# Mixer input tiles of a hybrid encoder trunk: three 256-wide products per weight block turned into one of 512 and one of 256, with the halves joined by ScalarE and VectorE

## The chip, the core and the metric

One core of a Trainium2 chip runs the whole kernel in one launch. The metric is the device time of an execution in microseconds (us). The engines are TensorE (PE, with its weight loads shown as PEld), VectorE (DVE), ScalarE (ACT), GpSimd (POOL) and SyncE (SP), which here only issues DMAs.

## The reference, cut to what matters

Two layers are computed over 256 tokens of 1024 channels. In each, the normalised input is projected once, and the columns of the projection feed attention (q, k, v), the Hyena mixer (`hy_in`) and the gates:

```
hn = rmsnorm(x, norm1_g[l])
proj = hn @ w_in[l]
q, k, v, hy_in, gates = jnp.split(proj, splits, axis=-1)
...
u = short_conv(hy_in, hy_conv_w[l], hy_conv_b[l])   # width 3, zero-padded at both ends
x0, x1, vv = jnp.split(u, 3, axis=-1); z = vv * x1
y = (fft_conv(z, h_fwd) + flip(fft_conv(flip(z), h_bwd)) + z * skip) ; b_out = y * x0
...
x = x + merged @ w_out[l]
x = x + peer(rmsnorm(x, norm2_g[l]), ...)
```

`hy_in` has 1536 channels, which are 12 tiles of 128. They alone are touched by the change.

## The kernel before, in words

All weights arrive as a stream of 128x1024 tiles through a ring of four slots. Products keep the accuracy of float32 by splitting both operands into a high and a low part: for every weight tile ACT writes the high half-tiles (`high_half`, called by `high_parts`, profile line L488), POOL subtracts to get the low ones (`low_parts`, L425), and PE then forms high x high, high x low and low x high. In `product` (L1449) these are three matmuls of 256 columns for each of the 8 blocks of a tile: L1452, L1454, L1456, so 24 in a tile. `contract` (L1462) does a tile and `project` (L1491) adds the wait for a free PSUM bank. `wide_tile` (L1472) is the other form, used before the change for the query tiles and the late expert tiles only: one matmul of 512 columns multiplies the high weights with the high and the low activations side by side (L1479), one of 256 adds low weights x high activations (L1481). It leaves the result in two halves of a bank, which somebody must add.

The order of the work is written out by hand on each engine, and each engine does its own list in order. The stretch that matters runs once a layer. PE's list is: 8 q/k tiles, the v tiles, then mixer tiles 0 and 1, `spread_scales`, mixer tiles 2 and 3, four matmuls for the filter taps (L1602), mixer tiles 4 to 6, four spectrum matmuls (L1613, the last of which waits for `bias_ready`), mixer tiles 7 and 8, the scores of heads 0 and 1 (`head_pair`, L1623), mixer tiles 9 to 11. After that comes a loop over 8 heads: gate tile 2h, a wait for the probabilities of head h, their four transposes (L1642), gate tile 2h+1, then either the scores of the next two heads or the product with the values (L1656). Later come the up projections, the output projection, the queries and the experts, which take most of the layer.

Tiles are numbered m for the banks: the mixer's tile n is m = 8 + n and lies in bank m % 4. A bank is free again when ACT has copied the tile four before it. ACT does this in `hyena_in` (L660), through `copy_tile` (L531, the copy is L534): wait for the tile on PE (`tile_wait`), make the high parts of the tile two ahead, then copy the 256 columns into `u_pad`, a buffer with a zero column at each end of a row. Between mixer tiles 9 and 10 ACT loads the table for Exp (L524) and between and behind tiles 10 and 11 it does the exponentials of heads 0 and 1 (`head_exp`, L698). In the gates' loop it takes a tanh of each gate tile out of its bank (L692).

DVE's list in this stretch is: w3 sums (L1063, L1064), `normalise_qk` for 4 pairs (L1045), the filters (L1072), the mask copied to PSUM (L1081) and added to the biases of 8 heads (L1083, then `bias_ready`), the spectrum (L1092, L1094), `conv(0)` and `conv(1)`, `head_scores` of heads 0 and 1 (L1110, L1114), `conv(2)` and `conv(3)`, then `normalise_probs(0)` (L1120, L1122), whose end releases the first transposes. The other eight convs stand between the heads behind it. A `conv` (L1096) is one TENSOR_SCALAR (L1100) and two SCALAR_TENSOR_TENSORs (L1102, L1104) on a row of `u_pad`, each waiting for the one before.

The code of the wait that sets when a mixer or gate tile may start:

```
def project(tile, m, wait=None, parts=(act_hi, act_lo)):
    if m >= 4:
        pe.wait_ge(tile_copied.sem, tile_copied.at(l, m - 3))
    contract(bank[m % 4][:, 0:S], 0, tile, wait=wait, parts=parts).then_inc(tile_done.sem, 1)
```

## Time and profile before

| | us |
|---|---|
| median of 3 runs | 2042.89 |
| lowest and highest | 2041.94, 2043.87 |
| the profiled execution, its own time | 2044.56 |
| the profiled execution, its span | 2042.7 |
| PE busy | 2032.7 of the span (100%) |
| PEld, POOL, DVE, ACT busy | 1807.5, 1605.7, 1278.4, 1079.1 |

The span runs from the first to the last instruction; the execution's own time is 1.86 us longer than its span. PE is busy throughout, so the time falls when PE's list gets shorter and rises with every wait that PE has to take. Matmuls overlap in the pipeline: one is recorded as 0.28 us long, while the next starts 0.12 us after it. What PE's work costs is therefore read from the distance between starts, not from the durations. Instructions of the other engines carry their duration, and a wait inside an instruction (for a port) makes it look longer.

### The profile page before, as it was taken

The page shows a single profiled execution, that of the slowest core. Times are in us where ns is not written, and L with a number is a line of the kernel's source. Part 1 is how long each engine was busy: PE and PEld are TensorE (multiplying, and loading weights), DVE is VectorE, ACT ScalarE, POOL GpSimd, SP SyncE. Part 2 cuts the span into 40 slices and gives each one's busy share as a digit, 9 for nine tenths or more (in the row PEclk, how much of TensorE's full clock was granted, in tenths as well). Part 3 has the DMA queues.
Part 4 walks back from the last instruction along what each step waited for, and adds up shares of the span by engine and source line. Part 5 has one row for each costly group of instructions (what it writes and reads, how often), then busy time and mean ns, then how long its engine had stood idle before and what let it go on. Part 6 is the DMA issues. An engine that isn't in the chain of part 4 may idle for free.

```text
span 2042.7 us, 43879 instructions
## 1 busy us (share of the span) xinstructions
PE 2032.7 (100%) x13412; PEld 1807.5 (88%) x13412; DVE 1278.4 (63%) x2655; ACT 1079.1 (53%) x2321; POOL 1605.7 (79%) x1316
## 2 busy tenths in 40 slices
PE   9999999999999999999999999999999999999999
PEld 8998899998888888888889898999988888888887
DVE  6776589778888333333377664996888873333333
ACT  6563654554444555555565546555444445555554
POOL 6776978887777888888877668788877778888886
PEclk9999999999999999999999999999999999999999
DMA  8543545554444555555684436555544445555554
GB/s 260 176 145 124 206 155 185 181 169 154 150 147 151 189 192 190 193 195 194 195 227 163 145 128 204 159 181 183 165 154 150 148 150 192 192 195 194 191 192 153
DMA packets 103393, 358.39 MB, mean 175 GB/s; under 512 B 11745, under 2 KB 16803, under 8 KB 103077
## 3 DMA queue, kind: packets, MB, share of 16 engines
q1 hardware_dynamic: 102612, 355.14, 53.1%
q10 hardware_dynamic: 720, 2.44, 0.4%
q8 instruction: 38, 0.62, 0.1%
q14 instruction: 23, 0.18, 0.0%
HBM read 356.49 MB, written 1.05 MB: 175 GB/s over the span
## 4 chain that ended last, share of the span: by engine, by line
PE 94%; DVE 3%; ACT 1%; POOL 1%; issue 1%; DMA 0%; SPq 0%; DVEq 0%; POOLq 0%; ACTq 0%
PE bank L1819 34%; PE bank L1479 15%; PE bank L1452 9%; PE bank L1456 9%; PE bank L1454 9%; PE bank L1481 8%; PE bank L1759 4%; POOL w_lo L425 1%; PE bank L1738 1%; PE bank L1699 1%; PE bank L1690 1%; DVE arena L1122 1%; DVE arena L1104 1%; DVE arena L1100 0%; ACT w_hi L488 0%
## 5 line engine op out<-in xcount | busy, mean ns | idle before, releaser
L425 POOL TENSOR_TENSOR w_lo<-ring,w_hi 128x512 fp32r<-128x512 f32 x1048 | 1404.1, 1356 | 345.8 <-ACT w_hi L488 345.2
L488 ACT ACTIVATE w_hi<-ring 128x512 fp32r<-128x512 f32 x1312 | 754.0, 621 | 377.7 <-PE bank L1456 326.9
L425 DVE TENSOR_TENSOR w_lo<-ring,w_hi 128x512 fp32r<-128x512 f32 x256 | 236.6, 924 | 450.2 <-ACT w_hi L488 450.0
L1452 PE MATMUL bank<-act_parts,w_hi 128*128 128x256 f32 x1600 | 458.9, 287 | 0.1
L1454 PE MATMUL bank<-act_parts,w_hi 128*128 128x256 f32 x1600 | 452.8, 283 | 0.0
L1456 PE MATMUL bank<-act_parts,w_lo 128*128 128x256 f32 x1600 | 452.7, 283 | 0.0
L1819 PE MATMUL bank<-w_hi,e_hi 128*128 128x512 f32 x1024 | 399.0, 390 | 0.2
L1819 PE MATMUL bank<-w_hi,e_lo 128*128 128x512 f32 x1024 | 398.5, 389 | 0.0
L1819 PE MATMUL bank<-w_lo,e_hi 128*128 128x512 f32 x1024 | 398.5, 389 | 0.0
L1479 PE MATMUL bank<-act_parts,w_hi 128*128 128x512 f32 x1088 | 385.9, 399 | 0.0
L1452 PEld LDWEIGHTS bank<-act_parts,w_hi 128*128 128x128 f32 x1600 | 306.9, 192 | 8.9 <-issue 7.2
L1454 PEld LDWEIGHTS bank<-act_parts,w_hi 128*128 128x128 f32 x1600 | 307.0, 192 | 1.0 <-issue 1.0
L1456 PEld LDWEIGHTS bank<-act_parts,w_lo 128*128 128x128 f32 x1600 | 306.9, 192 | 0.0
L1481 PE MATMUL bank<-act_parts,w_lo 128*128 128x256 f32 x1088 | 301.9, 277 | 0.0
L793 ACT ACTIVATE e_hi<-arena 128x256 fp32r (+1 forms) x256 | 106.8, 418 | 315.8 <-PE bank L1819 315.8
L453 POOL TENSOR_TENSOR e_lo<-arena,e_hi 128x256 fp32r<-128x256 f32 x256 | 190.8, 746 | 71.2 <-ACT e_hi L793 71.1
L1479 PEld LDWEIGHTS bank<-act_parts,w_hi 128*128 128x128 f32 x1088 | 204.1, 188 | 44.4
L1819 PEld LDWEIGHTS bank<-w_hi,e_hi 128*128 128x128 f32 x1024 | 192.2, 188 | 41.1 <-POOL e_lo L453 1.0
L1819 PEld LDWEIGHTS bank<-w_hi,e_lo 128*128 128x128 f32 x1024 | 192.2, 188 | 39.9
L1819 PEld LDWEIGHTS bank<-w_lo,e_hi 128*128 128x128 f32 x1024 | 192.2, 188 | 39.7
L1481 PEld LDWEIGHTS bank<-act_parts,w_lo 128*128 128x128 f32 x1088 | 204.6, 188 | 0.0
L799 ACT ACTIVATE norm_tmp<-bank 128x256 f32<-128x256 f32 x136 | 52.2, 384 | 238.7 <-PE bank L1481 238.7
(227 smaller groups left out, 2342.4 us busy)
## 6 DMA issues: line engine op xcount, KB each, us to landing
ring<-stream SPq DMA_DIRECT2D x654, 512.0 KB, 3.3
arena<-rpb_in SPq DMA_DIRECT2D x8, 512.0 KB, 7.9
arena<-dft_in SPq DMA_DIRECT2D x4, 512.0 KB, 6.0
arena<-subkeys ACTq DMA_DIRECT2D x2, 1024.0 KB, 7.0
xT<-x_in SPq DMA_DIRECT2D x4, 256.0 KB, 6.6
ring<-stream SPq DMA_DIRECT2D x4, 256.0 KB, 6.7
arena<-w_in SPq DMA_DIRECT2D x2, 512.0 KB
arena<-decay_in SPq DMA_DIRECT2D x2, 512.0 KB
```

Source lines behind the costliest of these rows:

```text
L425: eng.tensor_tensor(w_lo[:, part_, :], ring[:, tile % RING, half * HT:(half + 1) * HT], w_hi[:, part_, :].bitcast(F32), ALU.subtract).then ...
L453: pool.tensor_tensor(e_lo[:, n % AHEAD, :], experts[:, bass.ds(i * RING + n, 1), :].rearrange("p a t -> p (a t)"), e_hi[:, n % AHEAD, :].b ...
L488: nc.scalar.activation(w_hi[:, 2 * (tile % AHEAD) + half, :], ring[:, tile % RING, half * HT:(half + 1) * HT], ACT.Copy).then_inc(hi_ready ...
L793: nc.scalar.activation(e_hi[:, n % AHEAD, :], experts[:, bass.ds(i * RING + n, 1), :].rearrange("p a t -> p (a t)"), ACT.Copy).then_inc(e_ ...
L799: nc.scalar.activation(u_lo[:, n % 2, :], bank[n % 2][:, S:2 * S], ACT.Copy).then_inc(u_lo_ready.sem, 1)
L1452: T.matmul(out_, weights(w_hi, tile, j), hi[:, k, :], start=start, stop=False, skip_group_check=True)
L1454: T.matmul(out_, weights(w_hi, tile, j), lo[:, k, :], start=False, stop=False, skip_group_check=True)
L1456: return T.matmul(out_, weights(w_lo, tile, j), hi[:, k, :], start=False, stop=stop, skip_group_check=True)
L1479: T.matmul(out_[:, 0:2 * S], weights(w_hi, tile, k), both[:, :, k, :], start=(k == 0), stop=False, skip_group_check=True)
L1481: ins = T.matmul(out_[:, 0:S], weights(w_lo, tile, k), both[:, 0, k, :], start=False, stop=(k == KT - 1), skip_group_check=True)
L1759: ins = T.matmul(bank[2 + n % 2][:, t * NK:(t + 1) * NK], onehot_i[:, n % 2, t // 2, :, t % 2], weighted_j[:, n % 2, t // 2, c, :, t % 2], ...
L1819: ins = T.matmul(bank[4 + 2 * half + tt][:, :], e_[:, n % AHEAD, tokens], w_[:, part_, :], start=first and w_ is w_hi and e_ is e_hi, stop ...
```

## The change

Each of the 12 mixer tiles goes through `wide_tile` with both activation halves side by side. ACT, at the place where it copied the result, now copies the low half (columns 256 to 511 of the bank) into the row of `u_pad`. DVE gets 12 new instructions, `add_mix(n)`: wait for that copy, add the other half from PSUM onto the row. A bank of a mixer tile is free again when DVE has added, no longer when ACT has copied, and `conv(n)` waits for the add. The adds are put at fixed places of DVE's list: 0 and 1 ahead of `normalise_qk`, 2 and 3 behind it, 4 ahead of the mask, 5 between the biases of heads 4 and 5, 6 ahead of the spectrum, 7 behind `conv(0)`, 8 behind `conv(1)`, 9 behind `head_scores(1)`, 10 behind `conv(2)`, 11 behind `conv(3)`. `wide_tile` raises `tile_done` as `project` did.

```diff
--- before.py
+++ after.py
@@ -259,7 +259,9 @@
         ffn_done = sig("ffn_done", 2)
         arg_ready = sig("arg_ready", 2)
         sin_done = sig("sin_done", 2)
-        tile_copied = sig("tile_copied", 36)
+        tile_copied = sig("tile_copied", 24)
+        mix_low_ready = sig("mix_low_ready", 12)
+        mix_added = sig("mix_added", 12)
         q_lo_ready = sig("q_lo_ready", 2 * PH)
         q_sum = sig("q_sum", 2 * PH)
         q2_ready = sig("q2_ready", 2 * PH)
@@ -528,10 +530,11 @@
                     assert n_split[0] == tile + AHEAD
                     split_next()
 
-                def copy_tile(tile, m, dst):
-
-                    tile_wait(tile)
-                    nc.scalar.activation(dst, bank[m % 4][:, 0:S], ACT.Copy).then_inc(tile_copied.sem, 1)
+                def low_of_mix(n):
+
+                    tile_wait(T_HY + n)
+                    nc.scalar.activation(u_pad[:, n, 1:S + 1], bank[n % 4][:, S:2 * S], ACT.Copy
+                                         ).then_inc(mix_low_ready.sem, 1)
 
                 def raw_high(n, k, src):
 
@@ -658,7 +661,7 @@
                         norm_high(1, ((0,), (1, 2), (3,))[m - 4])
 
                 def hyena_in(n):
-                    copy_tile(T_HY + n, 8 + n, u_pad[:, n, 1:S + 1])
+                    low_of_mix(n)
 
                 def sine(n, dst):
                     act.wait_ge(arg_ready.sem, arg_ready.at(l, n))
@@ -1038,6 +1041,12 @@
                                        ).then_inc(v_scale_ready.sem, 1)
                 normalised(1, lambda s: None)
 
+                def add_mix(n):
+
+                    dve.wait_ge(mix_low_ready.sem, mix_low_ready.at(l, n + 1))
+                    row = u_pad[:, n, 1:S + 1]
+                    V.tensor_tensor(row, bank[n % 4][:, 0:S], row, ALU.add).then_inc(mix_added.sem, 1)
+
                 def normalise_qk(n):
 
                     dve.wait_ge(spread_done.sem, spread_done.at(l, n + 1))
@@ -1063,8 +1072,12 @@
                 V.tensor_tensor(w3_sd[:, 0, :], w3[:, 0, :], w3[:, 1, :], ALU.add)
                 V.tensor_tensor(w3_sd[:, 1, :], w3[:, 0, :], w3[:, 1, :], ALU.subtract
                                 ).then_inc(w3_ready.sem, 1)
+                add_mix(0)
+                add_mix(1)
                 for n in range(4):
                     normalise_qk(n)
+                add_mix(2)
+                add_mix(3)
 
                 for n in range(4):
                     sd, tt = n // TT, n % TT
@@ -1078,12 +1091,16 @@
 
                 dve.wait_ge(tables_in.sem, tables_in.at(l, tables_in.per_layer))
                 dve.wait_ge(filters_ready.sem, filters_ready.at(l, 4))
+                add_mix(4)
                 link(V.tensor_copy(mask_ps, mask))
                 for h in range(NH):
+                    if h == 5:
+                        add_mix(5)
                     ins = V.tensor_tensor(bias[:, h, :, :], bias[:, h, :, :],
                                           mask_ps.unsqueeze(1).to_broadcast([P, TT, S]), ALU.add)
                 ins.then_inc(bias_ready.sem, 1)
                 dve.wait_ge(bias_ready.sem, bias_ready.at(l, 1))
+                add_mix(6)
 
                 for ri in range(2):
                     dve.wait_ge(even_kept.sem, even_kept.at(l, ri + 1))
@@ -1095,7 +1112,7 @@
 
                 def conv(n):
 
-                    dve.wait_ge(tile_copied.sem, tile_copied.at(l, 8 + n + 1))
+                    dve.wait_ge(mix_added.sem, mix_added.at(l, n + 1))
                     w = C_CW + 3 * n
                     link(V.tensor_scalar(u[:, n, :], u_pad[:, n, 1:S + 1], col[:, w + 1:w + 2],
                                          col[:, C_CB + n:C_CB + n + 1], ALU.mult, ALU.add))
@@ -1126,11 +1143,16 @@
                     ins.then_inc(probs_ready.sem, 1)
 
                 conv(0)
+                add_mix(7)
                 conv(1)
+                add_mix(8)
                 head_scores(0)
                 head_scores(1)
+                add_mix(9)
                 conv(2)
+                add_mix(10)
                 conv(3)
+                add_mix(11)
                 tiles = [4, 8, 5, 9, 6, 10, 7, 11]
                 normalise_probs(0)
                 for p in range(NH // 2):
@@ -1488,11 +1510,24 @@
                         pe.wait_ge(raw_ready.sem, raw_ready.at(l, (n - 1) * KT + k + 1))
                     return wait
 
+                def bank_free(m):
+
+                    if 4 <= m < 12:
+                        pe.wait_ge(tile_copied.sem, tile_copied.at(l, m - 3))
+                    elif 12 <= m < 24:
+                        pe.wait_ge(mix_added.sem, mix_added.at(l, m - 11))
+                    elif m >= 24:
+                        pe.wait_ge(tile_copied.sem, tile_copied.at(l, m - 15))
+
                 def project(tile, m, wait=None, parts=(act_hi, act_lo)):
 
-                    if m >= 4:
-                        pe.wait_ge(tile_copied.sem, tile_copied.at(l, m - 3))
+                    bank_free(m)
                     contract(bank[m % 4][:, 0:S], 0, tile, wait=wait, parts=parts).then_inc(tile_done.sem, 1)
+
+                def mix_tile(n):
+
+                    bank_free(8 + n)
+                    wide_tile(bank[n % 4], 0, T_HY + n, both_acts)
 
                 def mean_square(n):
 
@@ -1583,15 +1618,15 @@
                             rows = slice(e * FFN, (e + 1) * FFN)
                             ins = T.matmul(bank[5][rows, 0:P], w2[rows, :], h1[rows, :], start=True, stop=True)
                         ins.then_inc(ffn_done.sem, 1)
-                project(T_HY, 8)
-                project(T_HY + 1, 9)
+                mix_tile(0)
+                mix_tile(1)
                 pe.wait_ge(qk_scale_ready.sem, qk_scale_ready.at(l, 1))
                 pe.wait_ge(arg_ready.sem, arg_ready.at(l, 2))
                 pe.wait_ge(v_ready.sem, v_ready.at(l, 2))
                 pe.wait_ge(taps_in.sem, taps_in.at(l, taps_in.per_layer))
                 spread_scales()
-                project(T_HY + 2, 10)
-                project(T_HY + 3, 11)
+                mix_tile(2)
+                mix_tile(3)
 
                 pe.wait_ge(sin_done.sem, sin_done.at(l, 2))
                 pe.wait_ge(w3_ready.sem, w3_ready.at(l, 1))
@@ -1602,7 +1637,7 @@
                     T.matmul(bank[4 + n][:, :], h2[rows, :], w3_sd[rows, sd, :], start=True, stop=True
                              ).then_inc(taps_done.sem, 1)
                 for n in range(4, 7):
-                    project(T_HY + n, 8 + n)
+                    mix_tile(n)
 
                 pe.wait_ge(filters_ready.sem, filters_ready.at(l, 4))
                 pe.wait_ge(tables_in.sem, tables_in.at(l, tables_in.per_layer))
@@ -1625,13 +1660,13 @@
                             if qt:
                                 ins.then_inc(scores_done.sem, 1)
 
-                project(T_HY + 7, 15)
-                project(T_HY + 8, 16)
+                mix_tile(7)
+                mix_tile(8)
                 pe.wait_ge(spec_ready.sem, spec_ready.at(l, 2))
                 head_pair(0)
-                project(T_HY + 9, 17)
-                project(T_HY + 10, 18)
-                project(T_HY + 11, 19)
+                mix_tile(9)
+                mix_tile(10)
+                mix_tile(11)
                 for h in range(NH):
                     project(T_GATE + 2 * h, 20 + 2 * h)
                     pe.wait_ge(probs_ready.sem, probs_ready.at(l, h + 1))
@@ -1670,7 +1705,7 @@
                     for j in (0, 1):
                         m = 2 * n + j
                         if m < 4:
-                            pe.wait_ge(tile_copied.sem, tile_copied.at(l, 36))
+                            pe.wait_ge(tile_copied.sem, tile_copied.at(l, 24))
                         else:
                             pe.wait_ge(up_used.sem, up_used.at(l, m - 3))
                         parts_ready(0, T_UP + n, j)
```

## Rows read from the trace of the kernel before

**Rows 1.** The page: busy time by engine, and the chain that ended last by engine

```profile
PE 2032.7 (100%) x13412; PEld 1807.5 (88%) x13412; DVE 1278.4 (63%) x2655; ACT 1079.1 (53%) x2321; POOL 1605.7 (79%) x1316
...
PE 94%; DVE 3%; ACT 1%; POOL 1%; issue 1%; DMA 0%; SPq 0%; DVEq 0%; POOLq 0%; ACTq 0%
```

**Rows 2.** Waits, 94.9 to 149.6 us: who, for whom, total, times, longest

```profile
PEld bank L1642 <- DVE arena L1122: 0.5, 2, 0.3
```

**Rows 3.** Timeline of PE: start, duration, line; narrow and wide tiles, scores, transposes

```profile
70.04 0.28 PE L1452 MATMUL bank<-act_parts,w_hi 128*128 128x256 f32 x1
...
72.92 3.60 PE L1613 MATMUL bank<-arena 128*128 128x512 f32 x8
...
94.88 0.60 PE L1642 MATMUL bank<-mats,arena 128*128 128x128 f32 x4
...
109.92 0.66 PE L1642 MATMUL bank<-mats,arena 128*128 128x128 f32 x4
...
221.96 0.40 PE L1479 MATMUL bank<-raw_parts,w_hi 128*128 128x512 f32 x1
...
224.73 0.40 PE L1479 MATMUL bank<-raw_parts,w_hi 128*128 128x512 f32 x1
```

**Rows 4.** Timeline of ACT: copies of mixer tiles 7, 9, 10 and 11

```profile
80.55 0.36 ACT L534 ACTIVATE arena<-bank 128x256 f32<-128x256 f32 x1
...
87.56 0.37 ACT L534 ACTIVATE arena<-bank 128x256 f32<-128x256 f32 x1
...
90.44 0.37 ACT L534 ACTIVATE arena<-bank 128x256 f32<-128x256 f32 x1
...
93.32 0.36 ACT L534 ACTIVATE arena<-bank 128x256 f32<-128x256 f32 x1
```

**Rows 5.** Timeline of DVE: an add from PSUM, biases, scores, convs 2 and 3, head 0

```profile
48.40 0.42 DVE L1058 TENSOR_TENSOR arena<-bank,norm_tmp 128x256 f32<-128x256 f32 x1
...
67.32 4.87 DVE L1083 TENSOR_TENSOR arena<-arena,bank 128x512 f32<-128x512 f32 x8
...
83.44 0.69 DVE L1110 SCALAR_TENSOR_TENSOR arena<-bank,arena 128x512 f32<-128x512 f32 x1 [1.66 <-PE bank L1623]
...
86.08 0.40 DVE L1100 TENSOR_SCALAR arena<-arena,cols_sb 128x256 f32<-128x256 f32 x1
86.52 0.48 DVE L1102 SCALAR_TENSOR_TENSOR arena<-arena,cols_sb 128x256 f32<-128x256 f32 x1
...
87.57 1.27 DVE L1100 TENSOR_SCALAR arena<-arena,cols_sb 128x256 f32<-128x256 f32 x1
88.87 1.40 DVE L1102 SCALAR_TENSOR_TENSOR arena<-arena,cols_sb 128x256 f32<-128x256 f32 x1
90.31 1.41 DVE L1104 SCALAR_TENSOR_TENSOR arena<-arena,cols_sb 128x256 f32<-128x256 f32 x1
92.03 0.17 DVE L1120 RECIPROCAL soft<-soft 128x2 f32<-128x2 f32 x1 [0.32 <-ACT arena L698]
92.23 2.18 DVE L1122 TENSOR_SCALAR arena<-arena,soft 128x256 f32<-128x256 f32 x2
```

**Rows 6.** Timeline of POOL: low parts of the weight tiles, 80 to 96 us

```profile
83.07 2.55 POOL L425 TENSOR_TENSOR w_lo<-ring,w_hi 128x512 fp32r<-128x512 f32 x2 [0.16 <-ACT w_hi L488]
87.21 8.35 POOL L425 TENSOR_TENSOR w_lo<-ring,w_hi 128x512 fp32r<-128x512 f32 x6 [1.59 <-ACT w_hi L488]
```

**Rows 7.** PE's clock: windows (busy, PEclk, DMA share, GB/s), then two matmuls of it

```profile
7.00:10.90 3.90, 2.24 (x16) 1.00 1.05 377
10.90:14.40 3.50, 3.16 (x15) 0.53 0.73 238
...
12.90 0.41 PE L1454 MATMUL bank<-raw_lo,w_hi 128*128 128x256 f32 x1
13.11 0.41 PE L1456 MATMUL bank<-raw_hi,w_lo 128*128 128x256 f32 x1
```

**Rows 8.** The second layer: head 0 on DVE

```profile
1105.97 0.17 DVE L1120 RECIPROCAL soft<-soft 128x2 f32<-128x2 f32 x1 [0.32 <-ACT arena L698]
```

## The prediction

> **What bounds the kernel now.** I read the page first, for who is busy and what chain ends last: PE is busy for 100% of the span and is 94% of the chain [rows 1]. So the time is PE's list plus PE's waits, and a change is worth what it takes out of or puts into those. Then I asked for the waits in the stretch around the change. Until the end of the mixer tiles PE has none that counts, and in the gates' loop it waits for DVE only twice, for 0.5 us together, 0.3 at most [rows 2]. Such a small wait in a stretch where DVE has no pause says the two are level: DVE delivers the probabilities just when PE comes for them. The timelines of PE, ACT, DVE and POOL [rows 3 to 6] then give the order of events, in microseconds of the first layer; the second repeats it, 1013.94 us later at head 0 (DVE starts head 0 at 92.03 and 1105.97, both times after 0.32 us of waiting [rows 5, 8]). I work out one layer and double it.
>
> **The gain on PE.** A narrow tile runs from 70.04 to 72.92, which is 2.88 us for 24 matmuls, 0.120 each [rows 3]. Eight steps of the wide form, one matmul of 512 columns and one of 256, take 224.73 - 221.96 = 2.77 us [rows 3]. Both stream 768 columns a step; the wide form saves one of three starts. So a mixer tile becomes 0.107 us shorter, twelve 1.28 us, both layers 2.57 us. That is the most that this change can win. It is 0.13%, under the 0.2% (4.1 us) that a measurement of this kernel can tell from no change.
>
> The Trainium skill, in "TensorE: Matmul & The Clock Gate", section "Back-to-back issue gap", gives 262 cycles of 2.4 GHz for 256 columns and 518 for 512, by which a step of three would cost 786 and one of two 780. By that page the gain would be 2.5 ns a step, 0.5 us in all; the trace's own pair says 13 ns a step, and the sum goes by the trace.
>
> **What ACT does.** Its copy has the same shape as before and stays where it was, so I cost it at nothing (bounds 0 to 0.05 us a tile, no row shows a copy of a bank's other half here). It comes earlier with PE's tiles: the copies end at 80.91, 87.93, 90.81 and 93.68 for mixer tiles 7, 9, 10 and 11 [rows 4], and move forward by 8, 10, 11 and 12 times 0.107, to 80.05, 86.86, 89.6 and 92.4.
>
> **What DVE does.** Each add reads 256 columns of PSUM and 256 of SBUF. The nearest row is the L1058 product, 0.42 us [rows 5]; the next instruction starts some 0.04 before such a one ends, so 0.38. Bounds are 0.38 and 1.40, which is what a 256-wide instruction on two SBUF tensors takes when POOL is at work (L1102) against 0.48 when it is not [rows 5]. I take 0.38, because the eight bias additions, one operand in PSUM too, take 0.61 each with no lengthening [rows 5]. The durations are small. What matters is that each add waits for ACT's copy of a tile, and everything behind it on DVE waits too.
>
> - Adds 0 to 3 delay `normalise_qk` and the filters by under 1 us each; PE comes for these several microseconds later. Nothing.
> - Adds 4 and 5 sit ahead of `bias_ready`. The biases ended at 72.19 [rows 5]. Add 4 can't start before the copy of tile 4, about 68.4, then come 0.4, the mask 0.45, 4.9 of biases and add 5: `bias_ready` at 74.5. PE needs it for the fourth spectrum matmul, at 72.92 - 0.75 + three quarters of 3.04 = 74.45 [rows 3]. A wait of 0 to 0.4; I take 0.1.
> - Add 6 is hidden before the spectrum, which waits for ACT and PE anyway.
> - Add 7 is where it turns. `conv(1)` used to run without waiting for tile 7. Now it stands behind add 7, which starts at 80.1. From here to the probabilities of head 0 DVE's list has no slack left.
>
> The list from 80.1: add 7 (0.4), `conv(1)`. Beside POOL an op is finished only when POOL's current one has ended, which made a conv of three ops 87.57 to 91.72 long, 4.15 us; `conv(2)`, in a gap of POOL, had its ops at 0.40 and 0.48 and is 1.45 long [rows 5]. For `conv(1)`, two of three met, I take 3.3: 83.8. Add 8: 84.2. Scores of heads 0 and 1, 86.08 - 83.44 = 2.64 [rows 5]: 86.8. Add 9 waits for ACT's copy at 86.86: 87.3.
>
> Now `conv(2)`. Before, it ran at 86.08 to 87.5, and POOL started a train of six low parts without a pause, 8.35 us, at 87.21 [rows 6]. That train moves forward by 10 x 0.107 to 86.1 and lasts to about 94.6. `conv(2)` at 87.3 falls into it: 3.3, to 90.6. Add 10: 91.0. `conv(3)`, also in the train: 3.3 to 4.15, I take 3.8: 94.8. Add 11: 95.1. Then head 0 as before, 0.17 and 2.18 with the start at 92.03 and the end at 94.41, so 2.38 [rows 5], less a little because the train is over: 97.2.
>
> **What PE does then.** It comes to the transposes of head 0 at 94.88 - 1.28 + 0.1 = 93.7 [rows 3] and starts them at 97.2, after 3.5 us of waiting. Against before it is 97.2 - 94.88 = 2.3 us late: the gain is gone and 2.3 more. Both bounds of this term: with every conv in a gap of POOL (1.45), and adds 10 and 11 then held by ACT's copies, the probabilities are there at 93.9 to 95.3, 1.0 early to 0.4 late; with both convs at 4.15 they come at 98.8, 3.9 late. I take 2.3 since POOL's train covers the whole stretch.
>
> Later heads: DVE was level with PE at head 2 (transposes at 109.92 [rows 3]). While PE stands, no new high parts are made and POOL falls idle, so the ops of the next convs drop from 1.40 to 0.48; five such are enough for DVE to be ahead by the next head. I cost them at nothing. If that cover is missing, the price is in rival C. Behind the gates' loop DVE waits for PE again, so nothing given away comes back.
>
> **PE's clock.** The granted clock is 1.00, the 2.4 GHz level, all along except once: after a stretch in which PE was busy for 2.24 of 3.90 us, it is 0.53 over 3.5 us, nearly all of that at the 1.2 GHz level, with matmuls 0.21 apart where they are 0.12 [rows 7]. That is 16 matmuls by 0.09, 1.4 us lost, in a place where PE had idled for only some 1.9 us. The new wait of 3.5 us is longer. So I expect one such drop behind it in each layer. Part of the slow time may fall into the wait; bounds 0 and 1.65 (3.5 x 0.47), I take 1.2.
>
> **The sum.** Per layer: -1.28 on PE's list, +3.6 of new waits (3.5 and 0.1), +1.2 of clock: +3.5. Two layers: +7.0. Against the profiled execution, span 2042.7 and own time 2044.56, that is 2049.7 and 2051.6; that execution stands 1.67 above the median of the runs, 2042.89, so the predicted median is 2049.9.
>
> **The rivals.**
>
> A. The wait comes, but the clock stays up. For it: the trace has one such drop only, at the start of the program, where other work ran. The sum is then +4.6 or a little over: 2047.5. With a drop in one layer only, 2048.7.
>
> B. Not slower. Place: `conv(2)` and `conv(3)`. If their ops fall between POOL's instead of behind them, the probabilities come by 93.9 to 95.3 as above. The point from which it decides is PE's new arrival, 93.7, for a gain, and 94.9 for no change. At the best the whole gain stays, 2042.9 - 2.4 = 2040.5; with one conv met and one not, about 95.3, +0.4 a layer, 2043.7. Against it: POOL's work per tile is two ops of 1.28 to 1.39 [rows 6], and a wide tile leaves 2.77 us, so it has hardly a gap.
>
> C. DVE stays the bound in the gates' loop. It reaches head 0 at 95.1 instead of 92.03, 3.1 late, and if all its later ops are as long as before, PE is 3.1 late from head 2 on: 2 x 3.1 + 2.4 for the clock, 2051.5. For it: the two waits of [rows 2]. Against it: the idle POOL.
>
> D. The wide product saves nothing in the mixer, as no wide tile runs there now. PE then delivers each tile later by up to 0.107 x n, the chain on DVE starts 0.8 later at add 7 and PE is 3.1 late: 2 x 3.1 + 2.4, 2051.5. The page named above would have it nearly so. Against it: the same form at 2.77 us in the query stage [rows 3].
>
> **How the numbers follow.** Forecast, wait and clock in both layers: 0.48. A, with the case of one drop: 0.27. B: 0.11. C: 0.06. D: 0.03. Something I have not seen, mostly worse (a second wait behind the first): 0.05. Faster by over 0.2% (below 2038.8) has no mechanism, since the gain ends at 2.6 us: 0.02. Within 0.2% (to 2047.0): B and the lower third of A, 0.20. Slower: 0.78. The range leaves out the gain of B and the far end: 2045.0 to 2052.3.
>
> **What would show it.** Right: PEld of L1642's line waits for DVE's L1122 once a layer for over 3 us, at head 0 and hardly at later heads; wide tiles start 2.77 us apart; `conv(2)` has ops of 1.4 where it had 0.48; the clock's row reads under 1.00 just behind the wait. Wrong: no wait at head 0 (B), waits at heads 2 and 4 as well (C), 2.88 between wide tiles (D), or a wait at the fourth spectrum matmul of over 0.5. If the wait is there and the clock reads 1.00, A holds.

## The result, and the profile after

The kernel after takes 2053.42 us (median of 5 runs, 2052.45 to 2055.66), the kernel before 2042.93 (5 runs, 2041.94 to 2043.87): 10.5 us more, ratio 1.0049 with a 95% interval of 1.0038 to 1.0060. The prediction was 2049.9 with a range to 2052.3. The sign and the mechanism are right, the size is not: the time lies 3.5 us over the forecast and 1.1 us over the end of the range.

The profiled execution of after has an own time of 2052.54 and a span of 2050.8, that of before had 2044.56 and 2042.7, so the two traces differ by 8.1 only. The other 2.4 us come from where the two executions lie among the runs: that of before stands 1.6 above the median of its kernel, that of after 0.9 under its own.

The busy line and the chain of the page of after, to be held against [rows 1]:

```profile
PE 2034.1 (99%) x13220; PEld 1801.2 (88%) x13220; DVE 1281.8 (63%) x2679; ACT 1079.6 (53%) x2321; POOL 1604.7 (78%) x1316
...
PE 96%; DVE 2%; ACT 1%; DMA 0%; issue 0%; POOL 0%; SPq 0%; DVEq 0%; ACTq 0%
```

PE has 192 matmuls fewer (eight for each of the 24 mixer tiles) and is nevertheless 1.4 us busier. A list that became shorter takes longer, so part of it ran slower. Where PE stood shows in its waits over the whole run (engine and line that waited, what it waited for: total, times, longest):

```profile
PEld bank L1677 <- DVE arena L1139: 8.0, 2, 4.0
...
PEld bank L1648 <- DVE arena L1099: 0.8, 2, 0.4
```

The first row answers to [rows 2]: L1677 are the transposes, L1139 the probabilities. They wait twice, once a layer and only at head 0, for 4.0 us each, where the first layer of before had 0.5 us in two waits at later heads. The second is a weight load of the fourth spectrum matmul, behind the biases and add 5. It waits 0.4 us a layer, but a load here starts 0.24 us after the one before it has ended in any case, and the matmuls lose nothing: from the first spectrum matmul to the next mixer tile it is 3.03 us (71.75 to 74.78), as it was 3.04 before.

Where the wait comes from is in DVE's timeline of the first layer (start, duration, engine, line; in brackets the idle time before it and what ended that). It answers to [rows 5]. L1048 is an add, L1117, L1119 and L1121 a conv, L1137 and L1139 head 0:

```profile
79.75 0.42 DVE L1048 TENSOR_TENSOR arena<-bank,arena 128x256 f32<-128x256 f32 x1 [1.52 <-ACT arena L536]
80.09 1.53 DVE L1117 TENSOR_SCALAR arena<-arena,cols_sb 128x256 f32<-128x256 f32 x1
81.65 0.48 DVE L1119 SCALAR_TENSOR_TENSOR arena<-arena,cols_sb 128x256 f32<-128x256 f32 x1
82.17 1.41 DVE L1121 SCALAR_TENSOR_TENSOR arena<-arena,cols_sb 128x256 f32<-128x256 f32 x1
...
86.58 0.41 DVE L1048 TENSOR_TENSOR arena<-bank,arena 128x256 f32<-128x256 f32 x1
86.92 1.53 DVE L1117 TENSOR_SCALAR arena<-arena,cols_sb 128x256 f32<-128x256 f32 x1
88.48 0.48 DVE L1119 SCALAR_TENSOR_TENSOR arena<-arena,cols_sb 128x256 f32<-128x256 f32 x1
89.00 1.40 DVE L1121 SCALAR_TENSOR_TENSOR arena<-arena,cols_sb 128x256 f32<-128x256 f32 x1
90.44 0.43 DVE L1048 TENSOR_TENSOR arena<-bank,arena 128x256 f32<-128x256 f32 x1
90.78 0.94 DVE L1117 TENSOR_SCALAR arena<-arena,cols_sb 128x256 f32<-128x256 f32 x1
91.75 1.40 DVE L1119 SCALAR_TENSOR_TENSOR arena<-arena,cols_sb 128x256 f32<-128x256 f32 x1
93.19 1.37 DVE L1121 SCALAR_TENSOR_TENSOR arena<-arena,cols_sb 128x256 f32<-128x256 f32 x1
94.59 0.42 DVE L1048 TENSOR_TENSOR arena<-bank,arena 128x256 f32<-128x256 f32 x1
94.94 0.15 DVE L1137 RECIPROCAL soft<-soft 128x2 f32<-128x2 f32 x1
95.12 1.98 DVE L1139 TENSOR_SCALAR arena<-arena,soft 128x256 f32<-128x256 f32 x2
```

From 79.75 DVE never stands. `conv(2)`, 1.45 us long before, takes 3.48 (86.92 to 90.40), and `conv(3)` 3.78. POOL's timeline beside it shows what they meet:

```profile
85.75 2.55 POOL L427 TENSOR_TENSOR w_lo<-ring,w_hi 128x512 fp32r<-128x512 f32 x2 [1.02 <-ACT w_hi L490]
88.57 8.38 POOL L427 TENSOR_TENSOR w_lo<-ring,w_hi 128x512 fp32r<-128x512 f32 x6 [0.28 <-ACT w_hi L490]
```

The first instruction of `conv(2)` ends at 88.45, 0.15 us behind POOL's pair (88.30); the second starts in POOL's pause of 0.28 us and takes 0.48; the third and all three of `conv(3)` lie in POOL's train of six, where they end 0.4 us behind one of its instructions (1.40 us each). The probabilities are ready at 97.10, where before had them at 94.41. PE at that moment (two rows of its timeline, the transposes of heads 0 and 1, with the first three matmuls between them):

```profile
97.16 1.11 PE L1677 MATMUL bank<-mats,arena 128*128 128x128 f32 x4 [3.78 <-DVE arena L1139]
97.92 0.56 PE L1474 MATMUL bank<-act_parts,w_hi 128*128 128x256 f32 x1
98.28 0.41 PE L1476 MATMUL bank<-act_parts,w_hi 128*128 128x256 f32 x1
98.50 0.41 PE L1478 MATMUL bank<-act_parts,w_lo 128*128 128x256 f32 x1
...
107.13 0.60 PE L1677 MATMUL bank<-mats,arena 128*128 128x128 f32 x4
```

Before, head 0 began at 94.88 and head 1 at 102.33, 7.45 us apart. Now the same work takes 107.13 - 97.16 = 9.97, and the matmuls start 0.21 apart. The windows of after say why (window, its length, then the busy time of PE, PEld, DVE, ACT and POOL, the granted clock, DMA's share and GB/s):

```profile
49.30:92.00 42.70, 42.70 (x245) 34.07 (x244) 34.60 (x56) 22.37 (x49) 31.93 (x26) 1.00 0.51 181
92.00:95.90 3.90, 1.37 (x12) 1.17 (x10) 3.76 (x6) 2.61 (x8) 3.90 (x4) 1.00 0.53 159
95.90:102.70 6.80, 5.54 (x26) 5.54 (x27) 4.66 (x10) 0.60 (x1) 1.05 (x1) 0.50 0.41 143
102.70:110.00 7.30, 7.30 (x61) 6.79 (x60) 3.95 (x7) 4.09 (x10) 4.45 (x4) 1.00 0.21 72
```

While PE stands, the granted clock goes from 1.00 to 0.50, which is from the 2.4 to the 1.2 GHz level, and stays there for 6.8 us, of which PE works 5.54. In before the same two windows read 1.00. The second layer is the same: a gap of 3.78, then

```profile
1114.90:1119.90 5.00, 4.98 (x24) 4.98 (x25) 3.42 (x9) 0.60 (x1) 0.00 (x0) 0.50 0.37 111
```

and 9.71 us from head 0 to head 1. So a layer's stretch, from the first matmul of the filter network (L1553 before, L1588 after) to the first matmul of the mixer's spectrum behind the gates' loop (L1690, L1725), goes from 118.25 to 123.09 us in the first layer and from 119.02 to 122.82 in the second: 8.6 us, and that is the whole difference between the traces but for 0.6 us at the program's start, where before ran its one stretch at 0.53 [rows 7] and after has none. Between the layers and behind them the two agree to 0.01 us.

### The profile page after: what moved, and what is told of

Its sections match the earlier page's. It is cut to its first block, busy times and chain, and to the rows that moved or that the text cites. A ratio compares the mean times of both kernels' runs of the same rounds, so it can differ in the third digit from the quotient of the medians.

```text
span 2050.8 us, 43521 instructions
## 1 busy us (share of the span) xinstructions
PE 2034.1 (99%) x13220; PEld 1801.2 (88%) x13220; DVE 1281.8 (63%) x2679; ACT 1079.6 (53%) x2321; POOL 1604.7 (78%) x1316
## 4 chain that ended last, share of the span: by engine, by line
PE 96%; DVE 2%; ACT 1%; DMA 0%; issue 0%; POOL 0%; SPq 0%; DVEq 0%; ACTq 0%
PE bank L1854 34%; PE bank L1501 17%; PE bank L1474 9%; PE bank L1478 9%; PE bank L1476 9%; PE bank L1503 8%; PE bank L1794 4%; PE bank L1773 1%; PE bank L1734 1%; PE bank L1725 1%; DVE arena L1121 0%; PE bank L1677 0%; PE bank L1607 0%; PE bank L1691 0%; DVE arena L1117 0%; PE bank L1609 0%
## 5 line engine op out<-in xcount | busy, mean ns | idle before, releaser
L1501 PE MATMUL bank<-act_parts,w_hi 128*128 128x512 f32 x1280 | 454.8, 399 | 0.0
L1474 PE MATMUL bank<-act_parts,w_hi 128*128 128x256 f32 x1408 | 404.8, 288 | 0.0
L1476 PE MATMUL bank<-act_parts,w_hi 128*128 128x256 f32 x1408 | 400.0, 284 | 0.0
L1501 PEld LDWEIGHTS bank<-act_parts,w_hi 128*128 128x128 f32 x1280 | 240.0, 188 | 55.9 <-issue 3.2
L1474 PEld LDWEIGHTS bank<-act_parts,w_hi 128*128 128x128 f32 x1408 | 272.1, 193 | 5.1 <-issue 4.8
L1476 PEld LDWEIGHTS bank<-act_parts,w_hi 128*128 128x128 f32 x1408 | 272.1, 193 | 0.5 <-issue 0.5
```

The costliest lines, as they stand in the source:

```text
L1474: T.matmul(out_, weights(w_hi, tile, j), hi[:, k, :], start=start, stop=False, skip_group_check=True)
L1476: T.matmul(out_, weights(w_hi, tile, j), lo[:, k, :], start=False, stop=False, skip_group_check=True)
L1501: T.matmul(out_[:, 0:2 * S], weights(w_hi, tile, k), both[:, :, k, :], start=(k == 0), stop=False, skip_group_check=True)
```

## The experiments

All medians are set against the kernel before on the same chip: 2043.92 us beside e1 to e4, 2044.73 beside e6, e10, e11 and e13, and 2043.75 beside e5, e9, e12 and e14. A ratio carries its 95% interval. Lines named with L are of the kernel that is spoken of.

**e4_wide_only: the wide product without adds.** Before, with the mixer tiles in the wide form, while ACT copies columns 0 to 255 and frees the bank as it did. It leaves out the product of the high weights and low activations in the mixer input.

```diff
+                def mix_tile(n):
+                    pe.wait_ge(tile_copied.sem, tile_copied.at(l, 5 + n))
+                    wide_tile(bank[n % 4], 0, T_HY + n, both_acts)
...
-                project(T_HY, 8)
-                project(T_HY + 1, 9)
+                mix_tile(0)
+                mix_tile(1)
...
```

> The kernel before, with the mixer tiles alone through the wide product; ScalarE copies columns 0 to 255 and frees the bank, nobody adds the other half, so the product of the high weights with the low activations is left out of the mixer's input. Theory T (the wide form is worth 0.107 us a tile, DVE's added list costs all the rest): 2042.9 - 2.6 = 2040.3, no wait at the head-0 transposes, and 2.77 us from wide tile to wide tile. Rival D (the wide form saves nothing here): 2042.9. Rival P (the wide tiles themselves bring something slow, in the banks or in the clock): over 2045.

Measured: 2041.33, 2.6 us under before, ratio 0.9987 (0.9978 to 0.9996). Head 0 starts at 93.24 without a gap. The interval allows 0.8 to 4.5 us, so the size is better read from the trace. Between the taps' first matmul (61.45) and the scores' (80.88) five tiles save 0.5 us against before. All twelve save 1.11 us of the way to head 0 in the first layer, which is 0.09 a tile, 12 ns a step and 2.2 us in two layers. The prediction had 0.107 a tile and 2.57. An estimate from the Trainium skill's figures ("TensorE: Matmul & The Clock Gate", section "Back-to-back issue gap"), which that section gives for the isolated gap, would have been 0.5 us; this trace doesn't bear it out. Rival D is out. The trace says one thing more: from the filter network to the last matmul before head 0, PE needs the same time in e4 as in after, to 0.02 us in the first layer. So neither the adds nor the banks that DVE frees hold PE up before head 0; all of the loss stands there and behind it.

**e11_adds_only: the adds without the wide product.** After, with the tiles narrow again; what is added is the copy of the same half, so the mixer input is doubled.

```diff
-                    nc.scalar.activation(u_pad[:, n, 1:S + 1], bank[n % 4][:, S:2 * S], ACT.Copy
+                    nc.scalar.activation(u_pad[:, n, 1:S + 1], bank[n % 4][:, 0:S], ACT.Copy
...
-                    wide_tile(bank[n % 4], 0, T_HY + n, both_acts)
+                    contract(bank[n % 4][:, 0:S], 0, T_HY + n).then_inc(tile_done.sem, 1)
```

> The changed kernel with the mixer tiles back at three matmuls of 256 columns; the adds, their waits and the bank releases by DVE stay. ScalarE copies and DVE adds the same columns, so the mixer's input is doubled. Theory T: PE comes 1.28 us later to everything per layer, and so does each copy on which DVE's list hangs, the gap at head 0 stays about 3.0 to 3.8 us with its low clock: 2043.9 + 2 x (3.3 + 2.5) = 2055.5, some 2 us above the changed kernel. Rival P (the wide tiles cause the low clock or the wait): 2043.9 to 2048.

Measured: 2053.49 (4 runs), 8.8 us over before, ratio 1.0041 (1.0025 to 1.0056), as slow as after within the intervals. The expectation was 2 us too high. PE comes 1.2 us later to head 0 (94.57) and the probabilities 1.0 later (98.1), so the gap is 3.56 instead of 3.79, and in the first layer the low clock held half as long (heads 0 and 1 are 8.99 apart, in the second layer 10.15). The adds in this order alone carry the loss; with them in place, what the wide form wins ends in the wait. This kernel has no wide tile in the mixer, and its second layer has a low stretch of 6.8 us, so the long stretches don't belong to the wide form either.

**e1_convs_late: two convs out of the way.** After, with `conv(2)` and `conv(3)` behind the last head's probabilities; their results are needed later still.

```diff
                 add_mix(9)
-                conv(2)
                 add_mix(10)
-                conv(3)
                 add_mix(11)
...
                         normalise_probs(2 * p + 2)
+                conv(2)
+                conv(3)
```

> The changed kernel with conv(2) and conv(3) moved from between the last adds to behind the probabilities of head 7, where DVE idles for 8.7 us. Theory T (DVE's list between mixer tile 7 and head 0 is what PE waits for, and the clock falls because of that wait): the adds 10 and 11 then only wait for ScalarE's copies, the probabilities come at about 93.5 to 94.5 instead of 97.1, PE waits under 1 us, the clock stays at 1.00: 2040.5 to 2042. Rival Q (the adds are slow wherever they are, or the banks freed by DVE hold PE): still above 2047.

Measured: 2042.98, ratio 0.9999 (0.9990 to 1.0008): the 10.5 us are gone, though it ends 1 us over what was expected. A gap of 1.07 is left in each layer, with the clock at 1.00 behind it. DVE's timeline shows what ends late now:

```profile
92.08 0.43 DVE L1048 TENSOR_TENSOR arena<-bank,arena 128x256 f32<-128x256 f32 x1 [2.29 <-ACT arena L536]
92.42 0.16 DVE L1137 RECIPROCAL soft<-soft 128x2 f32<-128x2 f32 x1
92.61 1.79 DVE L1139 TENSOR_SCALAR arena<-arena,soft 128x256 f32<-128x256 f32 x2
```

DVE is idle for 2.29 us ahead of add 11 and has head 0 behind it. The add waits for the copy of the last mixer tile, and PE is at the gate by then. That led to the next kernel.

**e10_head0_early: the best order.** As e1, with add 11 behind head 0's probabilities.

```diff
                 add_mix(9)
-                conv(2)
                 add_mix(10)
-                conv(3)
-                add_mix(11)
                 tiles = [4, 8, 5, 9, 6, 10, 7, 11]
                 normalise_probs(0)
+                add_mix(11)
...
                         normalise_probs(2 * p + 2)
+                conv(2)
+                conv(3)
```

> The changed kernel with conv(2) and conv(3) behind the probabilities of head 7, and add 11 behind those of head 0. In the run with the convs alone moved, head 0's probabilities waited for add 11 and that for ScalarE's copy (92.05), and PE still had a gap of 1.07 us there. Theory T: they now start at the end of the exponentials (90.4) and are there at about 92.9, before PE comes at 93.2; the gap goes, and the whole gain of the wide tiles stays: 2041.3 to 2042. Rival C (DVE is the bound at heads 2 and 4, whatever head 0 does): the gap moves there, 2043.

Measured: 2041.18 (11 runs), ratio 0.9986 (0.9977 to 0.9995), 3.6 us under before (the interval allows 1.0 to 4.7) and 12 us under the median of after. It beats both kernels. In its trace a layer's stretch is 117.11 and 117.30 us, about 1 us shorter than the 118.25 of before, as e4's 117.25 and 117.11. DVE's timeline and the transposes:

```profile
90.40 0.17 DVE L1137 RECIPROCAL soft<-soft 128x2 f32<-128x2 f32 x1 [0.70 <-ACT arena L701]
90.61 2.09 DVE L1139 TENSOR_SCALAR arena<-arena,soft 128x256 f32<-128x256 f32 x2
92.61 0.41 DVE L1048 TENSOR_TENSOR arena<-bank,arena 128x256 f32<-128x256 f32 x1
```

```profile
93.15 0.60 PE L1677 MATMUL bank<-mats,arena 128*128 128x128 f32 x4
```

The probabilities are there at 92.70, PE arrives at 93.15 and doesn't wait; its two windows behind that read busy throughout, at 1.00:

```profile
92.00:95.90 3.90, 3.90 (x35) 3.90 (x35) 3.83 (x5) 3.06 (x8) 3.60 (x4) 1.00 0.64 192
95.90:102.70 6.80, 6.80 (x57) 6.29 (x56) 6.55 (x10) 3.36 (x7) 4.97 (x4) 1.00 0.53 178
```

**e9_before_convs_late: the control.** Before, with the same two convs moved.

```diff
-                conv(2)
-                conv(3)
                 tiles = [4, 8, 5, 9, 6, 10, 7, 11]
...
                         normalise_probs(2 * p + 2)
+                conv(2)
+                conv(3)
```

> The kernel before, narrow tiles and no adds, with conv(2) and conv(3) behind the probabilities of head 7. It is the control for the version that was faster than both (wide tiles, adds, convs moved). Theory T: only the waits of 0.5 and 0.3 us at heads 2 and 4 can go: 0 to 0.8 us below the kernel before, so the wide tiles are what made that version faster. Rival V (moving the convs is the gain, the wide tiles bring nothing): about 2.5 below.

Measured: 2042.72, 1.0 us under before, ratio 0.9995 (0.9986 to 1.0004), which can't be told from no change; in its trace both layers take 118.25 us, as the first one of before. So the order alone doesn't make e10's gain; the wide tiles do, once the order lets them.

**e12_add7_later: is it add 7?** The prediction said that add 7 "is where it turns". After, with `conv(1)` ahead of it again.

```diff
                 conv(0)
-                add_mix(7)
                 conv(1)
+                add_mix(7)
                 add_mix(8)
```

> The changed kernel with add 7 behind conv(1) instead of ahead of it. The prediction said that from add 7 on DVE's list has no slack. In the trace of the changed kernel DVE did stand from 78.2 to 79.75 for it, but add 9 starts only at 86.58, right behind ScalarE's copy of tile 9 (86.46), while the scores ended at 86.67. Theory T2 (the list hangs on add 9 and ScalarE's copy, not on add 7): head 0 is there at 97.1 again, the time is that of the changed kernel. Rival T1 (add 7 starts the delay, as predicted): the probabilities come about 1 us earlier, 2 us less in all.

Measured: 2051.92, 8.2 us over before, ratio 1.0040 (1.0026 to 1.0054). The gap is 3.56 us in place of 3.79, no more. DVE's timeline, from add 7 to add 9:

```profile
80.33 0.48 DVE L1119 SCALAR_TENSOR_TENSOR arena<-arena,cols_sb 128x256 f32<-128x256 f32 x1
80.85 1.41 DVE L1121 SCALAR_TENSOR_TENSOR arena<-arena,cols_sb 128x256 f32<-128x256 f32 x1
82.30 0.42 DVE L1048 TENSOR_TENSOR arena<-bank,arena 128x256 f32<-128x256 f32 x1
84.07 0.43 DVE L1048 TENSOR_TENSOR arena<-bank,arena 128x256 f32<-128x256 f32 x1 [1.35 <-ACT arena L536]
...
88.11 0.42 DVE L1048 TENSOR_TENSOR arena<-bank,arena 128x256 f32<-128x256 f32 x1 [0.98 <-ACT arena L536]
```

`conv(1)` ran early and short, and the time won is spent standing before adds 8 and 9. Add 9 waits for ACT's copy of tile 9, and `conv(2)`, `conv(3)` and head 0 are behind it: from add 9 to the end of the probabilities it is 10.37 us here (88.11 to 98.48) and 10.52 in after (86.58 to 97.10). It turns at add 9. In after, that copy ended at 86.45, 0.13 us before DVE came, so both chains, that over add 7 and that over ACT, end there almost together.

**e2_gate_first: other work for PE in the wait.** After, with gate tile 1 ahead of head 0's transposes.

```diff
                     project(T_GATE + 2 * h, 20 + 2 * h)
+                    if h == 0:
+                        project(T_GATE + 1, 21)
                     pe.wait_ge(probs_ready.sem, probs_ready.at(l, h + 1))
...
-                    project(T_GATE + 2 * h + 1, 20 + 2 * h + 1)
+                    if h:
+                        project(T_GATE + 2 * h + 1, 20 + 2 * h + 1)
```

> The changed kernel with PE's list altered at one place: gate tile 1 is multiplied before the transposes of head 0 instead of behind them, so that PE has 2.9 us of work while DVE finishes the probabilities. DVE's list is untouched. Theory T: the probabilities still come at about 97, the wait shrinks from 3.8 to about 1 us, the clock stays up, and both the wait's and the clock's price go: 2041.5 to 2044. Rival R (the low clock is not caused by the wait): the low stretch stays, 2046.5 to 2049. Rival Q (adds and banks are slow everywhere): above 2049.

Measured: 2045.58, ratio 1.0007 (0.9998 to 1.0016): 1.7 us over before, 8 less than after, and 1.6 over the end of what was expected. In the profiled execution, which took 2048.00 and so 2.4 us more than the median, a gap of 0.98 is left (97.94 to 98.92), and a new one of 0.68 comes behind the transposes, where nothing covers ACT's copy of them any longer. In that execution the clock fell behind these two in the first layer, though not in the second.

**e13_busy_wait: a late head without an idle PE.** After, with 30 matmuls that nobody reads in the wait's place. It separates the lateness from the clock.

```diff
                     project(T_GATE + 2 * h, 20 + 2 * h)
+                    if h == 0:
+                        for _ in range(30):
+                            T.matmul(bank[7][:, 0:S], act_hi[:, 0, 0:P], act_hi[:, 0, :], start=True, stop=True)
                     pe.wait_ge(probs_ready.sem, probs_ready.at(l, h + 1))
```

> The changed kernel with 30 matmuls of 256 columns (act_hi by act_hi, into a bank that nobody reads then) put on PE's list between gate tile 0 and the wait for head 0's probabilities: 30 x 0.12 = 3.6 us of work in the place where PE stood for 3.8 us. DVE is untouched, so head 0 is as late as in the changed kernel. Theory T (the clock falls because PE stands still): the wait shrinks to 0.2, the low stretches go, and the time is that of the late head alone, about 2047.5 to 2049, with little scatter. Rival R (the low clock has another cause, the wide tiles or the load): low stretches stay, 2053.

Measured: 2048.88 (9 runs), ratio 1.0022 (1.0012 to 1.0032): 4.2 us over before (the interval allows 2.5 to 6.5). PE's timeline, the added matmuls and the transposes of heads 0 and 1, and a window of it:

```profile
93.13 3.76 PE L1674 MATMUL bank<-act_parts 128*128 128x256 f32 x30
97.17 0.66 PE L1680 MATMUL bank<-mats,arena 128*128 128x128 f32 x4 [0.28 <-DVE arena L1139]
...
104.67 0.60 PE L1680 MATMUL bank<-mats,arena 128*128 128x128 f32 x4
```

```profile
95.90:102.70 6.80, 6.52 (x53) 5.81 (x52) 5.48 (x12) 2.11 (x4) 2.27 (x2) 1.00 0.42 145
```

The probabilities are as late as in after (97.17 against 97.16), but the clock stays at 1.00 and head 1 follows in 7.50 us instead of 9.97. The late head costs 4.2 us; the other 5 to 6, up to the 10.5 and 9.3 by which after and its repeat e14 stand over before, go when PE is kept busy. In the trace a layer's stretch is 120.70 us, 2.45 over that of before, which is 4.9 in two. That is rival A made by hand: it said 2047.5, 4.6 over before.

**e5, e3, e6: how long must PE stand?** Before, with one, two or three reciprocals of a table that is free by then in DVE's list ahead of head 0, each 1.75 us and 1.79 to the next start. The diff is that of e3; e5 has a range of 1, e6 of 3.

```diff
                 conv(3)
+                for _ in range(2):
+                    link(V.reciprocal(norm_tmp[:, 0, :], norm_tmp[:, 1, :]))
                 tiles = [4, 8, 5, 9, 6, 10, 7, 11]
```

> The kernel before with one RECIPROCAL (1.75 us) in DVE's list behind conv(3), per layer, result unused: the small dose beside those of two (gap 2.3 us on PE) and three (3.9 us). Theory T: a gap of 0.6 to 1.2 us, no low stretch, 1.2 to 2.4 above the kernel before. Rival U (any new gap lets the clock fall): a low stretch in some executions, and a scatter like that of the run with two.

> The kernel before, with narrow tiles and no adds, and two RECIPROCALs on a spare SBUF row (1.75 us each) put into DVE's list behind conv(3), once per layer, results unused. It measures what a late head 0 costs by itself. Head 0 comes 3.5 us later and PE, which had about 0.45 us to spare, waits about 3.0 us per layer. Theory T: wait 3.0 and a low-clock stretch each, 3.0 + 2.5 = 5.5 per layer, 2054. Rival A (a wait costs its own length only): 2042.9 + 6.1 = 2049.0. Rival S (DVE gets faster again before PE needs it): under 2046.

> The kernel before with three RECIPROCALs (1.75 us each) in DVE's list behind conv(3), once per layer, results unused. With two, the gap on PE was 2.3 us and the profile showed one low stretch of 3.4 us in two layers. Theory T: the gap is about 4.0 us, as long as in the changed kernel, and now each layer has a low stretch, of up to 6.8 us: 2043.9 + 8.0 + 4 to 6 = 2056 to 2058. Rival A (a wait costs its length): 2051.9. Rival P (the long low stretches of the changed kernel belong to its wide tiles): one or no low stretch of 3.4 us, 2052 to 2054.

Measured: e5 2044.94, ratio 1.0006 (0.9997 to 1.0015); e3 2051.40, 1.0031 (1.0020 to 1.0042), with runs from 2047.22 to 2053.13; e6 2055.55, 1.0053 (1.0038 to 1.0068). Windows of e6, each layer's gap and the stretch behind it:

```profile
94.60:98.50 3.90, 0.03 (x1) 0.00 (x0) 3.76 (x6) 1.51 (x3) 2.98 (x3) 1.00 0.57 210
99.10:102.50 3.40, 3.40 (x18) 3.40 (x18) 2.88 (x8) 0.60 (x1) 0.00 (x0) 0.51 0.41 154
1114.70:1118.50 3.80, 0.00 (x0) 0.00 (x0) 3.66 (x6) 1.51 (x3) 2.90 (x3) 1.00 0.59 201
1119.70:1123.10 3.40, 3.40 (x18) 3.40 (x18) 2.31 (x7) 0.14 (x1) 0.00 (x0) 0.50 0.31 123
```

The narrow tiles of before pay for a gap of the same length too: heads 0 and 1 are 8.99 us apart, 1.54 more than before, as in e12 and in e14 below. The expectation had low stretches of up to 6.8 us for e6; both are 3.4. And e3, whose gap was 2.3 us and not the 3.0 expected, pays in its profiled execution in one layer only:

```profile
96.10:98.35 2.25, 0.00 (x1) 0.00 (x1) 2.15 (x5) 1.51 (x3) 1.89 (x3) 1.00 0.58 178
98.43:101.84 3.41, 3.41 (x17) 3.41 (x18) 3.23 (x7) 0.60 (x1) 0.99 (x1) 0.50 0.64 207
1114.20:1116.40 2.20, 0.01 (x1) 0.02 (x1) 2.10 (x5) 1.51 (x3) 1.87 (x3) 1.00 0.54 162
1116.40:1123.80 7.40, 7.40 (x60) 6.89 (x61) 7.00 (x14) 2.11 (x4) 3.75 (x3) 1.00 0.37 129
```

**e14_after_again: the kernel after, once more**, unchanged, in another set of runs, to see how much of it is the one profiled execution.

> The changed kernel once more, on the chip of the next three, since the kernel before has been at 2042.9, 2043.9 and 2044.7 in different sets of runs. Theory T (late head 0: 4.6 us; low clock behind it: 2 x 2.4): 9 to 10.5 above the kernel before of the same set. Rival A (the clock's part was chance): 4 to 6 above.

Measured: 2053.07 (5 runs), ratio 1.0046 (1.0033 to 1.0060). The gaps are 3.78 again, but the low clock held for 3.4 us in each layer instead of 6.8 (heads 0 and 1 are 8.87 and 8.99 apart). This trace also has a wait that after's profile lacks: in the second layer PE stood 1.9 us for a low part of POOL's, which hangs on ACT, which waited for a DMA of the weight stream (waits of e14, 1060 to 1073 us):

```profile
ACT w_hi L490 <- DMA ring<-stream: 7.2, 2, 4.1
...
PE bank L1501 <- POOL w_lo L427: 1.9, 1, 1.9
```

So the same total comes about in different ways. The gap is fixed; the low clock's length and delays ahead of the mixer vary from one execution to the next. Before's own profiled execution has such delays: 0.58 us at the program's start, against after's, and 1.00 in the second layer ahead of the mixer, of which 0.4 is a wait for a low part. Together that is the 1.6 us by which it stands over its median. After's has neither, so the 8.1 us between the two traces are too few: without these delays it would be some 9.6.

Side by side, from the profiled execution of each (us; first and second layer where they differ):

```
kernel   gap at head 0   low clock behind it   heads 0 to 1    median - before
e13      filled          none                  7.50            +4.2
e5       0.72            none                  7.50            +1.2
e1       1.07            none                  7.50            -0.9
e3       2.30            3.4 / none            9.04 / 7.49     +7.5
e12      3.56            3.4                   8.92 / 9.00     +8.2
e11      3.56            3.4 / 6.8             8.99 / 10.15    +8.8
e14      3.78            3.4                   8.87 / 8.99     +9.3
after    3.79            6.8                   9.97 / 9.71     +10.5
e6       3.91 / 3.88     3.4                   8.99 / 8.97     +10.8
```

## Why the prediction was right or wrong

- **The gain on PE: right, a little too large.** 2.57 us predicted, 2.2 in e4's trace.
- **ACT: right.** Copy 9 was put at 86.86 and ended at 86.45. This execution comes 0.58 us earlier into the whole stretch, so like for like it is 87.03, because the wide tiles save 0.09 each and not 0.107.
- **DVE's list: right, nearly step by step.** Each add was priced at 0.38 and takes 0.34 until the next instruction starts. Predicted and measured ends: `conv(1)` 83.8 and 83.58, the scores 86.8 and 86.67, `conv(2)` 90.6 and 90.40, `conv(3)` 94.8 and 94.56, head 0 97.2 and 97.10; with the 0.58 us by which this execution is ahead, DVE needed 0.4 to 0.5 us more than predicted. What carried it was reading two prices for the same conv [rows 5] as POOL's doing [rows 6]. Some of the closeness is luck: head 0 was put at a little under 2.38 "because the train is over", and it took 2.16 although POOL's train lasted to 96.95.
- **"Add 7 is where it turns": wrong as a cause.** With add 7 moved (e12) 0.23 us of a 3.79 us gap go. The list has a second chain, ACT's copy of tile 9 and what stands behind add 9. The number was right since both chains end within 0.13 us.
- **The spectrum wait: nothing.** 0.1 us a layer was taken. The weight load waits 0.4, and PE's matmuls lose nothing by it.
- **The wait at head 0: right, short by a half.** The prediction counted from where PE would have started the transposes to where it does: 3.5. Counted so, it is 3.95 (97.16 - 93.21, as the last matmul before started at 93.09 and the next would have come 0.12 later), and against e4 the way from the scores to head 0 is 3.97 longer. The gap of 3.79 is less because it begins at the end of the last matmul, which is 0.16 later.
- **Later heads: right that nothing is lost.** No wait of L1677 for L1139 is left at heads 1 to 7, so rival C is out. But DVE is so far ahead then that before's waits go too: from head 1 to the end of the stretch it is 51.58 where before had 52.12 and 51.89. The sum had not credited these 0.54 and 0.30 us.
- **The clock: the term that failed.** The prediction put 1.2 us a layer, with 1.65 as the upper bound, from the one low stretch of 3.5 us in before and with part of it falling into the gap. In after the stretch held 6.8 us; 5.58 us of it fell behind the gap in the first layer and 5.00 in the second, and cost 9.97 - 7.45 = 2.52 and 9.71 - 7.45 = 2.26. Both are 0.45 us per us at the lower level, the same as e6's 1.54 for 3.41. So the price per us was right and the length was wrong: one instance was taken for the size of the effect. Even the short stretch costs 1.5, since it began behind the gap in e6 and e14's second layer and nothing fell into the wait.

The sum of the first layer is then -1.11 (wide form) + 3.97 (wait) + 2.52 (clock) - 0.54 (waits of before that are gone) = 4.84, as in the traces (123.09 - 118.25). In the second layer the same sum gives 4.81 and the traces 3.80: before spent 1.00 us more there ahead of head 0 than in its first layer, and after did not. The prediction had +3.5 for each. Over both layers the sum is 9.65 where it had 7.0. The clock is short by 2.4 us, the wait by 0.9 and the wide form by 0.35; the spectrum gives back 0.2 and the later heads 0.8.

The forecast of the median was the median of before plus 7.0. With 9.65 in place of 7.0 it would have been 2052.5. The last 0.9 us to 2053.42 stay open, and they are within the noise: the interval of the 10.5 us goes from 7.8 to 12.3, and the repeat e14 is 9.3 over before.

What is shown: without the two convs ahead of head 0 the loss is gone (e1, e10), the adds without the wide tiles have it in full (e11), the wide tiles without adds have none of it (e4), and with PE busy in the wait 4.2 us are left of it (e13). That POOL lengthens the convs is read from the timelines alone; no run took POOL's work away. What stays open: why the low clock held 3.4 us in some layers and 6.8 in others. Gaps of 3.56 and 3.79 us were followed by both, and gaps of 3.9 by the short one. The delays ahead of the mixer in the second layer, in e14 behind a late DMA, were seen and not tested.

## What to carry to other kernels

An add that waits for another engine makes everything behind it in its queue wait too, so ask of each one what is needed next by the engine that sets the time, and put that first: here two convs that nobody needs before the last head is done, and an add whose bank PE wants a head later, stood ahead of the one item that PE was coming for. Moving them turned a change that loses 10.5 us into one that wins 3.6. Price a new gap on TensorE at its length plus what the clock takes behind it, here 1.4 to 2.7 us for each gap of 3.6 us or more, and if the gap can't be closed, look for work that can run in it.

## What the runs showed of the hardware that was not expected

- The granted clock fell behind every gap of 3.6 us or more at head 0 that was profiled (ten of ten layers), behind one of two gaps of 2.3, and behind none of the gaps of 0.7 and 1.1. In e2 it fell once behind two gaps of 0.98 and 0.68 with the transposes between them.
- Once fallen, it held for 3.4 or for 6.8 us, one length or its double, under the same kernel (after and e14). In after it fell while PE still stood (95.92, the gap ends at 97.16), in e6 0.6 us behind the gap's end.
- A low stretch took 1.4 to 2.7 us between heads 0 and 1 (e14 and e11), 0.45 us for each us of it that PE worked in.
- 30 matmuls in the gap, whose output nobody reads, brought the kernel from 10.5 and 9.3 us over before (after, e14) to 4.2 (e13).
- A 256-wide conv instruction of DVE takes 0.40 to 0.48 us or 0.94 to 1.53 beside POOL's low parts, while an add with one operand in PSUM takes 0.41 to 0.43 in the same stretches.
